# Two more loads into the place of expert 0's fourth weight unit, and five experts of TensorE's loop written out

## What is computed

```python
gu = xb @ w1[e] + b1[e]
gate = jnp.minimum(gu[:, :F], SWIGLU_LIMIT)
up = jnp.clip(gu[:, F:], -SWIGLU_LIMIT, SWIGLU_LIMIT)
act = (up + 1.0) * gate * jax.nn.sigmoid(SWIGLU_ALPHA * gate)
return act @ w2[e] + b2[e]
```

## Time and profile before

| | |
|---|---|
| median of 3 runs | 1227.49 us (1227.3 to 1229.3) |
| the profiled execution's own time | 1227.92 us |
| its span, first to last instruction | 1225.9 us |
| mean granted TensorE clock | 0.999 |
| PE busy | 1169.0 us (95%) |
| HBM read | 459.19 MB, 375 GB/s over the span |
| instruction packets of queue q8 | 24, 0.39 MB |

### The profile page before, as it was taken

One profiled execution on the slowest core, in us unless ns is written; L12 is line 12 of the kernel. 1 busy time (PEld: TensorE's weight loads), 2 busy tenths in 40 slices (PEclk: granted clock), 3 DMA queues, 4 the chain that ended last, 5 costly groups with the idle time before them and its releaser, 6 DMA issues.

```text
span 1225.9 us, 17199 instructions
## 1 busy us (share of the span) xinstructions
PE 1169.0 (95%) x7154; PEld 588.0 (48%) x7154; DVE 428.0 (35%) x741; ACT 207.7 (17%) x306; POOL 58.5 (5%) x43
## 2 busy tenths in 40 slices
PE   9999999999999999999999999999999899999897
PEld 8888888888643334333333333333333333333332
DVE  5886764655632223222222222222222222222222
ACT  6444553534400000000000000000000000000001
POOL 0850000000300000000000000000000000000000
PEclk9999999999999999999999999999999999999999
DMA  9756437877889999999999999999999999999996
GB/s 310 272 207 217 161 138 258 317 283 320 337 350 428 431 433 433 429 431 434 433 430 430 433 433 432 429 433 434 432 429 433 433 433 428 433 433 434 428 423 255
DMA packets 47522, 461.79 MB, mean 377 GB/s; under 512 B 4985, under 2 KB 6978, under 8 KB 32290
## 3 DMA queue, kind: packets, MB, share of 16 engines
q1 hardware_dynamic: 44760, 458.97, 89.9%
q10 hardware_dynamic: 2730, 2.36, 0.7%
HBM read 459.19 MB, written 1.07 MB: 375 GB/s over the span
## 4 chain that ended last, share of the span: by engine, by line
PE 66%; DMA 32%; DVE 1%; SPq 1%; ACT 0%; issue 0%; DVEq 0%; ACTq 0%
PE ps L1289 19%; DMA w_ring<-in_w 19%; PE ps L1355 12%; DMA A_QK<-in_w 6%; DMA xb_and_att<-in_w 6%; PE ps L1006 4%; PE ps L1444 4%; PE ps L1014 3%; PE ps L1012 3%; PE ps L1013 3%; PE ps L1263 2%; PE ps L1007 2%; PE ps L1026 1%; PE ps L1139 1%; PE ps L1141 1%; PE ps L1140 1%
## 5 line engine op out<-in xcount | busy, mean ns | idle before, releaser
L1289 PE MATMUL ps<-w_ring,A_W 128*64 128x512 f32 x1216 | 272.5, 596 | 28.9 <-DMA w_ring<-in_w 28.4
L1890 DVE TENSOR_SCALAR A_W<-ps 128x512 f32<-128x512 f32 x32 | 22.1, 692 | 478.2 <-PE ps L1289 478.2
L1289 PEld LDWEIGHTS ps<-w_ring,A_W 128*64 128x64 f32 x1216 | 84.8, 137 | 200.9 <-issue 160.2
L1355 PE MATMUL ps<-w_ring,A_W 128*64 128x512 f32 x608 | 137.9, 595 | 0.0
L1534 DVE TENSOR_TENSOR w_parts<-w_ring,w_parts 128x1024 fp32r<-128x1024 f32 x76 | 109.9, 1463 | 56.4 <-ACT w_parts L733 55.5
L1289 PE MATMUL ps<-A_QK,A_W 128*64 128x512 f32 x416 | 93.2, 595 | 9.3 <-DMA A_QK<-in_w 9.3
L918 ACT ACTIVATE A_W<-ps 128x512 f32<-128x512 f32 x31 | 18.5, 597 | 462.9 <-PE ps L1336 462.9
L1289 PE MATMUL ps<-xb_and_att,A_W 128*64 128x512 f32 x384 | 86.2, 596 | 9.4 <-DMA xb_and_att<-in_w 9.4
L733 ACT ACTIVATE w_parts<-w_ring 128x1024 fp32r<-128x1024 f32 x75 | 78.9, 1058 | 64.6 <-PE ps L1007 32.1
L914 ACT ACTIVATE A_W<-A_W 128x512 f32<-128x512 f32 x32 | 20.2, 631 | 359.8 <-DVE A_W L1890 359.8
L1006 PE MATMUL ps<-hT_both,w_parts 128*128 128x512 f32 x224 | 79.3, 399 | 0.0
(11 more groups left out here) (266 smaller groups left out, 1198.7 us busy)
## 6 DMA issues: line engine op xcount, KB each, us to landing
w_ring<-in_w SPq DMA_DIRECT2D x110, 2048.0 KB, 35.2
A_QK<-in_w SPq DMA_DIRECT2D x38, 2048.0 KB, 35.1
xb_and_att<-in_w SPq DMA_DIRECT2D x35, 2048.0 KB, 35.2
w_ring<-in_w_in SPq DMA_DIRECT2D x36, 1024.0 KB, 7.3
w_ring<-in_w SPq DMA_DIRECT2D x8, 1024.0 KB, 23.7
w_ring<-in_w_ret_branch SPq DMA_DIRECT2D x2, 2048.0 KB, 10.9
xb_and_att<-in_w SPq DMA_DIRECT2D x4, 1024.0 KB, 20.6
A_W<-in_w_out SPq DMA_DIRECT2D x1, 2560.0 KB, 13.0
```

The costliest lines, as they stand in the source:

```text
L1289: mm = pe.matmul(o, XT[:, k, :], hidden_columns(tile[:, j, :], c), start=(k == 0), stop=(k == KC - 1))
L1355: mm = pe.matmul(ps[CAP * c:CAP * c + CAP, 3, :], lhs, w2_tile(flat)[:, q % W2_ROWS, c * HALF:(c + 1) * HALF], start=False, stop=(q == FQ ...
L1890: dve.tensor_scalar(gl, bank(0), LIMIT, None, ALU.min).then_inc(s.g, 1)
```

## The change

The place of unit 3 is used twice more: for unit 14 (w2 of expert 1, first unit) and, when that is used, for unit 24 (w1 of expert 4, third unit). Both leave the order of the ring (`ring_order`), so that units 15 to 23 stand one place earlier in it than before, and units from 25 on two. `freed_at(n)` gives the count of used units at which the place of unit n is free: for units 15 to 23 n - 10 instead of n - 9; for unit 25 14 instead of 16; for the pairs 26 and 27 to 32 and 33 one less than before; from unit 34 on n - 9 as before. Unit 14 is issued in two halves, behind those of units 11 to 13: the first when the first row of unit 3 is used (for which `hidden_first` now counts that row in `s_wu` too), the second when unit 3 is used. Unit 25 is issued ahead of unit 24, which waits until unit 14 is used. The semaphore of the place is `s_unit[3]`, so later waits on it count further (`UNIT_BASE`).

For PE the pair and the count of a unit's wait are no longer the same in the first round of the loop as in the others. So the first five experts are written out ahead of the loop, with constants in their waits, and the loop runs five rounds instead of six. The work of an expert and its order are the same.

```diff
+        ONE_SHOT = A_W[:, 0:UNIT_WORDS]
+        ONE_SHOT_UNITS = {14: 48, 24: 64}
+        UNIT_BASE = [16, 16, 16, 64]
+
+        def ring_order(n):
+            return n - (n > 14) - (n > 24)
+
+        def freed_at(n):
+
+            q = ring_order(n) - RING
+            return q + (q >= 14) + (q >= 23) + 1
...
         def place(n):
 
-            pair, upper = n // 2 % (RING // 2), n % 2
+            if n in ONE_SHOT_UNITS:
+                return ONE_SHOT, s_unit[3], ONE_SHOT_UNITS[n]
+            q = ring_order(n)
+            pair, upper = q // 2 % (RING // 2), q % 2
             flat = pairs[pair][:, upper * UNIT_WORDS:(upper + 1) * UNIT_WORDS]
-            return flat, s_pair[pair], 32 * (n // RING + (pair >= 2)) + (16, 32, 0, 0, 0)[pair]
+            return flat, s_pair[pair], 32 * (q // RING + (pair >= 2)) + (16, 32, 0, 0, 0)[pair]
...
-                for one in range(2):
-                    if n + one > RING + HALF_UNITS:
-                        sp.wait_ge(s_used, used + n + one - RING + 1)
+                for one in ((1, 0) if n in ONE_SHOT_UNITS else (0, 1)):
+                    if n + one in ONE_SHOT_UNITS:
+                        sp.wait_ge(s_used, 14 + 1)
+                        load_w1(sp, e, u + one, n + one)
+                    elif n + one > RING + HALF_UNITS:
+                        sp.wait_ge(s_used, freed_at(n + one))
                         load_w1(sp, e, u + one, n + one)
...
             for u in range(W2_UNITS):
-                sp.wait_ge(s_used, used + n + u - RING + 1)
-                load_w2(sp, e, u, n + u)
+                if n + u not in ONE_SHOT_UNITS:
+                    sp.wait_ge(s_used, freed_at(n + u))
+                    load_w2(sp, e, u, n + u)
...
+            sp.wait_ge(s_wu, OUT_DONE + W1_UNITS)
+            sp.dma_start(w2_tile(ONE_SHOT)[:, 0:2, :], w2_source(1, 0)[:, 0:2, :]).then_inc(s_unit[3], 16)
+            sp.wait_ge(s_used, W1_UNITS)
+            sp.dma_start(w2_tile(ONE_SHOT)[:, 2:4, :], w2_source(1, 0)[:, 2:4, :]).then_inc(s_unit[3], 16)
             for i in range(1, TURN):
                 load_expert_w1(sp, i + 1, i + 1, 0)
                 load_expert_w2(sp, i, i, 0)
...
-                    hidden_unit(first_units[u], u, s_wu if u < HALF_UNITS else None).then_inc(s_used, 1)
+                    hidden_unit(first_units[u], u, s_wu).then_inc(s_used, 1)
...
-            with pe.Fori(0, (N_EXP - 2) // TURN) as r:
-                rounds = r * (16 * TURN * E_UNITS // RING)
+
+            def expert(i, k, rounds):
...
+            for k in range(TURN):
+                expert(k, k, 0)
+            with pe.Fori(1, (N_EXP - 2) // TURN) as r:
                 for k in range(TURN):
...
+                    expert(r * TURN + k, TURN + k, (r - 1) * (16 * TURN * E_UNITS // RING))
```

More of the change, by code:

```diff
@@ L450, in load_expert_w1 @@
                 if n >= FIRST_PAIR:
-                    pair = n // 2 % (RING // 2)
+                    pair = ring_order(n) // 2 % (RING // 2)
                     to, source = pairs[pair].rearrange("p (j n) -> p j n", j=PAIR_ROWS), w1_both(e, u)
-                    sp.wait_ge(s_used, used + n + 1 - RING + 1)
+                    sp.wait_ge(s_used, used + freed_at(n + 1))
                     for odd in range(2):
@@ L606, in _ @@
                 n = w1_number(N_EXP - 1, u)
-                sp.wait_ge(s_used, n - RING + 1)
+                sp.wait_ge(s_used, freed_at(n))
                 sp.dma_start(w1_tile(place(n)[0]), w1_source(N_EXP - 1, u)).then_inc(s_unit[u], 16)
             for n, (e, u) in enumerate(((N_EXP - 2, 0), (N_EXP - 2, 1), (N_EXP - 1, 0))):
-                sp.wait_ge(s_used, w2_number(e, u) - RING + 1)
+                sp.wait_ge(s_used, freed_at(w2_number(e, u)))
                 flat = place(w2_number(e, u))[0]
@@ L614, in _ @@
                     sp.dma_start(w2_tile(flat)[:, rows, :], w2_source(e, u)[:, rows, :]).then_inc(s_w2half[2 * n + h], 16)
-            sp.wait_ge(s_used, N_UNITS - 1 - RING + 1)
+            sp.wait_ge(s_used, freed_at(N_UNITS - 1))
             for j in range(W2_ROWS):
@@ L1327, in hidden_extra @@
                 for u in range(W1_UNITS):
-                    pe.wait_ge(s_unit[u], i * 16 + 48)
+                    pe.wait_ge(s_unit[u], i * 16 + UNIT_BASE[u] + 32)
                     hidden_unit(w1_part(u), u).then_inc(extra.w1_used, 1)
@@ L1378, in hidden_last @@
                 for u in range(W1_UNITS):
-                    pe.wait_ge(s_unit[u], 32)
+                    pe.wait_ge(s_unit[u], UNIT_BASE[u] + 16)
                     hidden_unit(place(w1_number(N_EXP - 1, u))[0], u).then_inc(s_used, 1)
@@ L1484, in _, with transpose_previous @@
             pe.wait_ge(s_res, 2 * TT)
-            with pe.Fori(0, (N_EXP - 2) // TURN) as r:
-                rounds = r * (16 * TURN * E_UNITS // RING)
-                for k in range(TURN):
[L1488 to L1500, removed]
+            def expert(i, k, rounds):
+                def transpose_previous():
+                    pe.wait_ge(main.swe, i + 1)
+                    transpose_act(main, i)
+                hidden(i + 1, w1_number(k + 1, 0), rounds, transpose_previous)
+                pe.wait_ge(main.ate, i + 1)
+                pe.wait_ge(main.ye, i + 1)
+                gather(main, i + 2)
+                scatter(main, i)
+                pe.wait_ge(main.x, i + 3)
+                project_down(i, w2_number(k, 0), rounds)
+            for k in range(TURN):
+                expert(k, k, 0)
+            with pe.Fori(1, (N_EXP - 2) // TURN) as r:
+                for k in range(TURN):
+                    expert(r * TURN + k, TURN + k, (r - 1) * (16 * TURN * E_UNITS // RING))
             pe.wait_ge(s_table, 1)
```

## The result

The changed kernel takes **1232.77 us** (1232.05 to 1233.51, 6 runs) against 1227.45 (1227.2 to 1229.3, 6 runs): ratio 1.004, interval 1.0028 to 1.0051. It is 5.3 us slower where 4.8 us faster was forecast. The profiled execution took 1232.65 us with a span of 1230.6, 4.7 more than before.

A forecast was written before the change was run, and what follows sets the result against it. The weight stream was taken to bound the kernel; closing its gap gains one unit, 4.85 us, all else costing 0: span 1225.9 to 1221.0, time 1223.1, less 0.43 for the runs' median, 1222.7 us; range 1220.8 to 1225.2.

The forecast's parts named there:

- What bounds the kernel, and the gap: Weight stream sets the end; from 339.5 to 344 us it stands idle because SP waits for a free place.
- no step at units 34 to 37: Rival at these loads: over 10.45 us to first landing hands gain back; at half the gain 1225.1 us; chance 0.05.
- the tight load: First load of units 36 and 37: landed 15.3 us after issue, forecast 10.45 after the change, without running dry.
- the sum: Total of all terms: -4.85 us, one unit of stream gained from units 14 to 33, every other part costing 0.
- PE's written-out pass: "I take 0": PE at 470 to 602 us: new code fetched in about 6 more packets, taken to cost the stream 0.
- unit 23's late landing: Upper bound on a code packet's price: landings 5.73 us apart for 4.85, so up to 0.9 each, 5.4 in all.
- Rival (b): Jump back after each later pass: loop code no longer held, 24 further packets at 0.9 us, 1249.7 us; chance 0.03.
- PE's first wait for a load: PE's timeline: first wait for a load later by 1.7 experts, near 660 us.

The follow-up runs named there:

- e1_pad: The changed kernel with 67 instructions of long-fulfilled waits ahead of PE's loop, its head at 247 again as before the change; 1225.64 us, ratio to before 0.9984.
- e7_pad40: The changed kernel with 40 instructions of long-fulfilled waits ahead of PE's loop, head at 220; 1225.63 us, one run.
- e5_pe_only_pad: The kernel before with only PE's first five experts written out, old loads, plus 67 instructions of padding ahead of the loop; 1228.64 us, ratio 1.001.
- e2_pe_only: The kernel before with only PE's part of the change, the first five experts written out, and the old loads; 1236.42 us, ratio 1.0073.
- e4_no_loop: The changed kernel with all thirty experts of PE's loop written out, so nothing jumps back; 1231.89 us, ratio 1.0032.
- e6_short_body: The changed kernel, unpadded, with 64 instructions less per expert (two of three gather parts left out, so not a usable version); 1224.16 us, ratio 0.9968.
- e8_pad107: The changed kernel with 107 instructions of long-fulfilled waits ahead of PE's loop, head at 31; 1236.31 us, one run.
- e3_before_pad: The kernel before with 128 instructions of padding ahead of its loop, head moved from 247 to 119; 1252.39 us, ratio 1.0204.

## Why the prediction was wrong

**What bounds the kernel, and the gap.** Right in kind, and the term too large. The stream sets the end, and the gap was SP waiting for a place. All landings around it came within about 1 us, and no step at units 34 to 37 gave it back (9.9 us for the tight load). Where the sum has 4.85, the engines' idle time in the gap fell by 3.5 us, from 4.92 to 1.40. PE's unit 3 took 5.35 us for 3.65, so unit 4 ended and unit 15 left 1.0 us later than forecast: from 334 to 338 us the granted clock was 0.64, part of the stretch at the lower of its levels, 1.2 GHz. It was 0.62 there in e1_pad, where 1.54 us of idle time are left, and 1.00 in e7_pad40, where 0.36 are. Nothing here shows what made it fall.

**PE's written-out pass: "I take 0".** The first step that failed, by its price. The 6 packets were 7, at 470 to 602 us, where they were forecast. Their price was read from 400 to 500 us, where three packets left the rate at 432 GB/s. At 0.1 us each three packets take 0.3 us of 100, 1.3 GB/s, hardly more than such a row can show, and it shows the mean of the engines alone. Measured, they cost 0.9 us in e5_pe_only_pad. The other end, 0.9 from unit 23's late landing, was of the right kind and too large: one engine falls back, and the load waits for it.

**Rival (b), "the body is as long as before, and it was held for five passes".** The step that failed and that made the sign: it was given 0.03. Being held is not a property of the length alone, but of length and place, and the change moved the place by 1725 instructions. What (b) said then happened: fetches in each pass, and a stall behind the jumps. The earlier trace rows did not show one, because before the body was held. The Trainium skill (Runtime: NRT & Kernel Launch, Instruction fetch mechanics) expects such a fetch for a taken branch out of the window; the trace agrees, with 3.5 to 3.7 us of idle time at three jumps. (b)'s 30 packets became 43 (67 - 24), and its 0.9 us each became about 0.2. That is still nearly what it needed to decide (0.25 for 30): 43 packets at the 0.20 to 0.23 us of the table below lose 8.5 to 10 us, against 3.5 to 4 us won, which leaves 4.5 to 6.5 where 5.3 was measured.

**The price of a packet.** Each pair of kernels that differ in the code alone gives one, from the times against their own before:

| pair | packets more | us more | us each |
| --- | --- | --- | --- |
| after and e1_pad | 36 | 5.32 + 1.78 = 7.10 | 0.20 |
| e2_pe_only and e5_pe_only_pad | 36 | 9.00 - 0.87 = 8.13 | 0.23 |
| e4_no_loop and e1_pad | 27 | 4.47 + 1.78 = 6.25 | 0.23 |
| e5_pe_only_pad and before | 7 | 0.87 | 0.12 |

The first three hold what the stores at the end cost too. Up to PE's last matmul their profiled executions differ by 6.41, 6.28 and 4.59 us, 0.17 to 0.18 a packet.

The mechanism shows best in e6_short_body, where a single packet lies alone. From 363 to 368.5 us q8 moves one:

```profile
q8 instruction: 1, 0.02, 1.2%
```

The loads' completions around it, by engine (the 16 of a load in the order in which they come):

```
first engine  fifteenth  last engine  last - first
      359.39     361.13       362.37          2.98
      364.28     366.03       368.81          4.52
      369.17     370.92       373.71          4.54
      374.07     375.80       378.60          4.54
```

In the load in which it falls fifteen engines end 4.9 us behind the load before, as in the others, and the last one 6.44. Its lag stays 1.54 us larger from there on: **one packet sets one engine of 16 back by about 1.5 us, for good**. Spread over all engines that is 1.54 / 16 = 0.096 us, the 0.10 of the ledger.

The rest of the 0.2 is that the packets don't fall on all of them. One pair of places is loaded anew every 48.6 us, by two DMAs; here are two such loads, twelve rounds apart, as means of the first eight and of the last eight of their 32 completions, with the q8 packets since 341 us:

```
             packets  first eight  last eight
before             6       554.72      561.13
                   6      1137.57     1143.91
after             12       560.75      567.76
                  49      1143.53     1157.66
e4_no_loop        11       560.43      567.38
                  39      1143.21     1155.51
```

In all three kernels the first eight come 582.8 us later, to 0.1 us, whether no packet passes or 37. The last eight take 582.8 us before, 589.9 in the changed kernel and 588.1 in e4_no_loop: 7.1 us for 37 packets and 5.4 for 28, and 1.54 / 8 x 37 = 7.1, 1.54 / 8 x 28 = 5.4. So **the fetches fall on eight of the sixteen engines, at 1.54 / 8 = 0.19 us of delay a packet**, and every load waits for these eight. Which eight the records don't tell. The Trainium skill (Runtime: NRT & Kernel Launch, Instruction fetch mechanics) calls the cost of crossing a 16 KiB boundary of code "mostly hidden"; for PE that holds (no stall in e4_no_loop), for a stream that fills all engines it does not (4.5 us lost there).

**PE's first wait for a load** came at 716.38 and not near 660: a wrong forecast without a cost. PE was 4.9 us later at 606.91 than at 601.97 before, 3.74 of it the first stall, and at 2.9 us an expert that is 1.7 experts of 29.1 us more. e1_pad has no stall but its padding, 4.07 us, and the same wait at 715.19. PE time of these passes is not in the total, as the prediction said.

**The padded version.** e1_pad is 2.9 us above the forecast of 1222.7. Seven packets with the second pass take 0.9 (e5_pe_only_pad) to 1.4 (at 0.2), and the gap gave back 3.4 us (4.92 to 1.54) for 4.85, 1.5 less: 2.4 to 2.9 in all. The gain of the two loads themselves, with the code held, is 0.87 + 1.78 = 2.65 us of 4.85, where the idle time in the gap differs by 2.96 (4.50 in e5_pe_only_pad); unheld, 3.7. The one run of e7_pad40, with 0.36 us of idle time left, is no faster than e1_pad (1225.63), and that stays open; its engines are 5.15 us apart at the end where e1_pad's are 3.3.

## What to carry to other kernels

Where a loop's code is almost as large as what the engine holds, any edit ahead of it or in it, even of an instruction that does nothing, can turn fetching on or off for every pass: count the code packets by stretch before and after, and ask of a written-out pass first where it moves the loop. Price such fetches by completions of the single DMA engines and not by a rate: in a stream that fills all of them each fetch here cost 0.1 us of the mean rate, and 0.2 of the time, because eight of the engines bore it. A few instructions of padding where the engine has time to spare, or a shorter body, can cost less than the fetches (7.1 us here); too much padding starves the stream, as in e8_pad107.

## What the runs showed of the hardware that was not expected

- 1738 instructions of a loop (6.8 pieces of 256) were held over four or five passes with the head at 220 or 247 of 256, and fetched anew at each pass, 8 or 9 pieces of it, at 31, 119 and 180. That fits seven pieces held and eight not, if the pieces begin elsewhere than the program's count has it (by that count alone the places 220 and 247 would touch eight and 31 seven). The offset was not measured, so seven and eight are a reading and not shown; a body of 1420 instructions (head at 52) was held too.
- Waits that are already fulfilled cost PE idle time that grows faster than their number: 1.13 us for 40 instructions (e7_pad40), 4.07 for 67 (e1_pad), 8.49 for 107 (e8_pad107), 0.11 us for each further one; 13.33 for 128 in e3_before_pad. They too stand as "issue", and so look like a stall for code.
- The code packets of q8 delayed eight of the sixteen DMA engines by 1.54 us each time and never the other eight (582.8 us for twelve rounds with and without packets).
- The granted clock fell behind PE's stalls: 0.98 and 0.97 in the two stretches from 600 to 800 us of the changed kernel, 1.00 as the mean from 600 to 1180 in e4_no_loop, which has none (means over stretches in which either level can stand). It cost nothing, since the stream sets the end.
